# A conformer convolution stage: first projection with its output channel by channel, taps from its second block on, a layer norm of other pieces

## The chip, the cores and the metric

The kernel runs on one core of a Trainium2 chip. The metric is the device time of one execution in microseconds (us); the median of some executions is compared. The engines are named as the profile names them: PE (TensorE, its weight loads PEld), DVE (VectorE), ACT (ScalarE), POOL (GpSimd), SP (SyncE, which issues most DMAs).

## The reference, cut to what matters

A trunk of two layers works on 256 positions of 1024 channels in float32: retention and a dense SwiGLU in layer 0, a conformer convolution module and a mixture of eight experts in layer 1. The change is in the convolution module:

```python
def conv_module(h, w_pw1, b_pw1, w_dw, b_dw, ln_g, ln_b, w_pw2, b_pw2):
    a = h @ w_pw1 + b_pw1
    u = a[..., :D_MODEL] * jax.nn.sigmoid(a[..., D_MODEL:])
    u = lax.conv_general_dilated(
        u, w_dw[:, None, :], window_strides=(1,), padding=[(CONV_WIDTH - 1, 0)],
        dimension_numbers=('NWC', 'WIO', 'NWC'), feature_group_count=D_MODEL) + b_dw
    ...
    un = ((uf - mu) * lax.rsqrt(var + EPS) * ln_g.astype(jnp.float32) + ln_b.astype(jnp.float32)).astype(h.dtype)
    return jax.nn.silu(un) @ w_pw2 + b_pw2
```

`w_pw1` is 1024 x 2048, `w_pw2` 1024 x 1024, the depthwise convolution is causal with 31 taps per channel, and `mu` and `var` run over the 1024 channels of a position.

## The kernel before, in words

Every weight matrix streams through SBUF in blocks of 1 MB (128 partitions x 2048 floats). SP loads a block into one of six `raw` buffers (`load`, L283), as soon as `lo` has freed it. ACT rounds it to fp32r (`hi`, L411, into one of three `whi`), DVE takes the difference (`lo`, L706, into `wlo`). Activations are split in the same way into `xh` and `xl`. A product is then three matmuls: hi by hi, lo activation by hi weight, hi activation by lo weight. `hi` waits until PE has finished the block three before it. Each engine's program is a list written out by hand; engines meet at semaphores, so the place of a `hi`, a `lo` or a tap in its engine's list decides when it runs.

The convolution module, in order:

- `residual(2)` and `turn(2)` normalise and transpose the input; `xh_evac` and `xl_evac` make `xh` and `xl` (512 columns at a time, four of each).
- First projection: blocks `B_PW1` to `B_PW1+7`. `columns` (L1176) keeps a piece of `xh` or `xl` as the stationary operand and streams 512 columns of weights, so the output has positions on partitions. 24 matmuls a block.
- `glu(half)` (L928), after four blocks each: DVE adds the bias to the gate (L932) and to the value (L935), ACT takes the sigmoid (L558), DVE multiplies (L939). PE transposes the product to channels on partitions (`u_turn`, L1439), ACT copies it to `uT` (L564).
- Taps: a chunk is 128 channels. DVE does one tap of one chunk per instruction over 256 positions (`tap`, L956 and L958): chunks 0 to 2, 22 taps of chunk 3 and 21 of chunk 4. PE does the other 112 taps as matmuls with a diagonal of weights (L1455), which ACT builds (L578) into eight buffers. DVE adds the two parts of chunks 3 and 4 (L980). `lo` of the first three blocks of the second projection stands between the taps.
- Layer norm over channels: PE sums `y` with a matrix of ones (L1463), DVE scales the mean (L983) and subtracts it (L985), ACT squares (L600), PE sums the squares the same way (L1467), DVE takes the diagonal of the result and scales it (L988 to L991), POOL takes the power -1/2 (L369), ACT builds two diagonals (L603), PE spreads them over the partitions (L1471), DVE multiplies (L994), ACT does Silu with gain and bias (L606) and copies to `xh` (L608), DVE makes `xl` (`vl`, L905).
- Second projection: `rows` (L1187, L1196, L1197, L1203), four blocks of 24 matmuls of 512 columns; per tile t, hi parts and then lo parts. A block waits for two chunks of `xl` (L1474). In the last block `half_down` is signalled when tile 0 is complete.
- `residual(3)` (L859):

```python
                for t in range(TILES):
                    if t == 0:
                        dve.wait_ge(half_down, n)
                    else:
                        dve.wait_ge(pe_done, used)
                    ...
                        last = nc.vector.tensor_tensor(res[:, t, cols], banks[t][h][:, :], res[:, t, cols], ALU.add)
                    last.then_inc(res_done, 1)
                    if t == 0:
                        mean_square(n, 0)
```

`mean_square` (L711) waits for ACT's sum of squares (L404). Behind it come the normalisation, the transposes (L1267), the router (L1485, matmuls of 8 columns) and the experts, whose rows are gathered by matmuls with a one-hot matrix of 128 columns (L1501, L1502).

## Time and profile before

| | |
|---|---|
| median of 3 runs | 1724.94 us (1723.87 to 1728.66) |
| the profiled execution | 1721.76 us, of which the span of the profile is 1720.0 us |
| busy: PE, PEld | 1619.3 us (94%), 1311.2 us (76%) |
| busy: DVE, ACT, POOL | 1250.5 us (73%), 1024.5 us (60%), 161.6 us (9%) |
| from HBM | 448.61 MB, 261 GB/s over the span |
| mean granted clock of TensorE | 0.978 |

Busy time is the share of the whole span; the convolution module lies between about 467 and 608 us. A matmul's end is modelled, so the distance between the starts of two matmuls says more than the duration of one. The granted clock is given in parts of the full level, 2.4 GHz; 0.50 is the lower level, 1.2 GHz. The trace leaves out some records, so counts in a short stretch can be a little low, and a float32 matmul has two records. The time of the profiled execution holds 1.76 us that lie around its span.

### The profile page before, as it was taken

The page shows a single profiled execution, that of the slowest core. Times are in us where ns is not written, and L with a number is a line of the kernel's source. Part 1 is how long each engine was busy: PE and PEld are TensorE (multiplying, and loading weights), DVE is VectorE, ACT ScalarE, POOL GpSimd, SP SyncE. Part 2 cuts the span into 40 slices and gives each one's busy share as a digit, 9 for nine tenths or more (in the row PEclk, how much of TensorE's full clock was granted, in tenths as well). Part 3 has the DMA queues.
Part 4 walks back from the last instruction along what each step waited for, and adds up shares of the span by engine and source line. Part 5 has one row for each costly group of instructions (what it writes and reads, how often), then busy time and mean ns, then how long its engine had stood idle before and what let it go on. Part 6 is the DMA issues. An engine that isn't in the chain of part 4 may idle for free.

```text
span 1720.0 us, 20864 instructions
## 1 busy us (share of the span) xinstructions
PE 1619.3 (94%) x7325; PEld 1311.2 (76%) x7326; DVE 1250.5 (73%) x1024; ACT 1024.5 (60%) x872; POOL 161.6 (9%) x83
## 2 busy tenths in 40 slices
PE   8999989999899779989999999999999899999996
PEld 6887778888788667767788878878888777777774
DVE  6745554544569559979998888845555499999996
ACT  4344343443349438768777777744444487878874
POOL 0000000000000005006040040010000040330000
PEclk9999999999999869999999999999999899999998
DMA  9653545555442018999999989937666499999994
GB/s 348 208 195 99 182 165 190 195 172 194 175 169 74 25 44 328 393 357 365 397 370 394 371 287 390 373 130 243 207 205 202 148 360 395 374 396 395 375 395 183
DMA packets 191589, 450.23 MB, mean 262 GB/s; under 512 B 8493, under 2 KB 9021, under 8 KB 191422
## 3 DMA queue, kind: packets, MB, share of 16 engines
q1 hardware_dynamic: 189068, 444.83, 71.8%
q10 hardware_dynamic: 2482, 4.85, 0.8%
q8 instruction: 28, 0.46, 0.1%
q14 instruction: 11, 0.09, 0.0%
HBM read 448.61 MB, written 1.05 MB: 261 GB/s over the span
## 4 chain that ended last, share of the span: by engine, by line
PE 63%; DVE 16%; DMA 11%; issue 6%; ACT 3%; DVEq 0%; POOL 0%; ACTq 0%; SPq 0%; POOLq 0%
PE bank L1173 13%; PE bank L1166 12%; PE bank L1167 12%; DVE wlo L706 9%; DMA raw<-in_moe_w_down 6%; DMA raw<-in_moe_w_gu 5%; PE bank L1244 4%; PE bank L1196 3%; PE bank L1203 3%; PE bank L1197 3%; ACT whi L411 3%; DVE y L958 2%; PE bank L1235 2%; PE bank L1236 2%; PE bank L1233 1%
## 5 line engine op out<-in xcount | busy, mean ns | idle before, releaser
L706 DVE TENSOR_TENSOR wlo<-raw,whi 128x2048 fp32r<-128x2048 f32 x422 | 959.6, 2289 | 304.5 <-ACT whi L411 304.1
L411 ACT ACTIVATE whi<-raw 128x2048 fp32r<-128x2048 f32 x422 | 806.5, 1916 | 434.8 <-PE bank L1173 261.9
L1166 PE MATMUL bank<-whi,xx 128*128 128x512 f32 x1152 | 459.2, 399 | 15.1 <-DVE xx L1082 8.7
L1167 PE MATMUL bank<-whi,xx 128*128 128x512 f32 x1152 | 452.8, 393 | 0.0
L1173 PE MATMUL bank<-wlo,xx 128*128 128x512 f32 x1488 | 403.9, 393 | 6.3 <-DVE wlo L706 6.1
L1173 PEld LDWEIGHTS bank<-wlo,xx 128*128 128x128 f32 x1488 | 277.8, 189 | 75.0 <-DVE wlo L706 17.7
L1166 PEld LDWEIGHTS bank<-whi,xx 128*128 128x128 f32 x1152 | 219.5, 191 | 62.2 <-issue 11.2
L1167 PEld LDWEIGHTS bank<-whi,xx 128*128 128x128 f32 x1152 | 219.2, 190 | 44.2
L378 POOL TENSOR_SCALAR onehot<-mats,slot 128x64 fp32r<-128x64 f32 x56 | 150.4, 2709 | 757.9 <-PE bank L1508 757.9
L1244 PE MATMUL bank<-wlo,hT 128*128 128x512 f32 x504 | 143.8, 407 | 16.7 <-DVE wlo L706 14.3
L1244 PEld LDWEIGHTS bank<-wlo,hT 128*128 128x128 f32 x504 | 90.5, 189 | 59.1 <-DVE wlo L706 42.5
L507 ACT ACTIVATE hT<-bank 128x512 fp32r<-128x512 f32 x77 | 44.2, 593 | 96.4 <-PE bank L1385 55.0
L1233 PE MATMUL bank<-whi,hT 128*128 128x512 f32 x336 | 92.3, 397 | 4.4 <-DVE hT L891 4.4
L1164 PE MATMUL bank<-whi,xx 128*128 128x512 f32 x336 | 90.1, 390 | 0.0
L891 DVE TENSOR_TENSOR hT<-bank,hT 128x512 fp32r<-128x512 f32 x77 | 51.5, 683 | 41.5 <-ACT hT L507 41.4
L1233 PEld LDWEIGHTS bank<-whi,hT 128*128 128x128 f32 x336 | 63.3, 190 | 19.3 <-issue 3.8
L1164 PEld LDWEIGHTS bank<-whi,xx 128*128 128x128 f32 x336 | 63.1, 188 | 13.4
L885 DVE TENSOR_TENSOR hid<-bank,sgate 128x512 f32<-128x512 f32 x77 | 51.5, 684 | 20.6 <-PE bank L1173 20.6
L1235 PE MATMUL bank<-whi,hT 128*128 128x512 f32 x168 | 65.9, 392 | 0.0
L1236 PE MATMUL bank<-whi,hT 128*128 128x512 f32 x168 | 65.8, 392 | 0.0
L354 POOL TENSOR_TENSOR rstd<-ms,mhalf 128x1 f32<-128x1 f32 x10 | 6.0, 598 | 513.1 <-DVE ms L711 513.1
L958 DVE SCALAR_TENSOR_TENSOR y<-uT,wdwT,y 128x256 f32<-128x256 f32 x131 | 52.4, 475 | 0.0
(214 smaller groups left out, 1294.3 us busy)
## 6 DMA issues: line engine op xcount, KB each, us to landing
raw<-in_moe_w_gu SPq DMA_DIRECT2D x224, 1024.0 KB, 8.2
raw<-in_moe_w_down SPq DMA_DIRECT2D x112, 1024.0 KB, 8.6
raw<-in_ffn_w_gu SPq DMA_DIRECT2D x28, 1024.0 KB, 5.1
raw<-in_ret_w_in SPq DMA_DIRECT2D x24, 1024.0 KB, 7.2
raw<-in_ffn_w_down SPq DMA_DIRECT2D x14, 1024.0 KB, 4.9
raw<-in_conv_w_pw SPq DMA_DIRECT2D x12, 1024.0 KB, 5.1
raw<-in_ret_w_out SPq DMA_DIRECT2D x8, 1024.0 KB, 4.9
res<-in_x SPq DMA_DIRECT2D x2, 512.0 KB, 4.1
```

Source lines behind the costliest of these rows:

```text
L378: last = nc.gpsimd.tensor_scalar(onehot[:, n // 2, at_:at_ + HALF], iota[:, h * HALF:(h + 1) * HALF], slot[:, e + 1, n, h:h + 1], None, AL ...
L411: nc.scalar.activation(whi[base % SPLIT][:, :], raw[base % RAW][:, :], ACT.Copy).then_inc(hi_done, 1)
L706: nc.vector.tensor_tensor(wlo[base % SPLIT][:, :], raw[base % RAW][:, :], whi[base % SPLIT][:, :].bitcast(f32), ALU.subtract).then_inc(lo_ ...
L958: ins = nc.vector.scalar_tensor_tensor(y[:, c, :], uT[:, c, k:k + SEQ], w, y[:, c, :], ALU.mult, ALU.add)
L1164: nc.tensor.matmul(dst[:, :], xmix[:, kc, t, :], wh, start=kc == 0, stop=False)
L1166: nc.tensor.matmul(dst[:, :], xh[:, kc, t, :], wh, start=kc == 0, stop=False)
L1167: nc.tensor.matmul(dst[:, :], xl[:, kc, t, :], wh, start=False, stop=False)
L1173: last = nc.tensor.matmul(dst[:, :], both, wl, start=False, stop=closing and kc == DC - 1)
L1233: nc.tensor.matmul(dst, hTmix[:, kc, t, :], wh, start=False, stop=False)
L1235: nc.tensor.matmul(dst, hTh[:, kc, t, :], wh, start=False, stop=False)
L1236: nc.tensor.matmul(dst, hTl[:, kc, t, :], wh, start=False, stop=False)
L1244: last = nc.tensor.matmul(dst, both, wl, start=False, stop=stop and c == 1)
```

## The change

- The first projection keeps a 128 x 128 piece of the weights stationary and streams the 256 positions of `xh` or `xl` (`channels`), so its output has channels on partitions. A pair of blocks gives four chunks of output, two of values and two of gates, in four banks; the loads are cut in two so that a block holds both. A block is 48 matmuls of 256 columns. The first waits for all four pieces of `xh`, and for `xl` only after its first 16 matmuls.
- The transposes, the copies to `uT`, the bias broadcast and the bias adds go. ACT takes the sigmoid from PSUM with the bias as its operand; DVE adds the bias, multiplies, and writes `uT` in one instruction per chunk (`glu`). These happen per pair of blocks.
- DVE takes whole chunks 0 to 4 (155 taps), PE whole chunks 5 to 7 (93 taps). DVE's first taps come after `glu(0)`; its order of taps, `lo` and `glu` is new. The three `lo` of the second projection move from between the taps to behind them: `lo(B_PW2)` before the mean, the next two between the multiplies of the layer norm.
- Layer norm: the sums use a matrix of 1/D, four of the eight mean sums are made during PE's taps, DVE subtracts straight from PSUM. For the variance the squares are the stationary operand and one column of 1/D streams. A one-element Silu is placed ahead on ACT.
- Second projection: the matmuls of a block are ordered by chunk, hi parts of both tiles first and lo parts last, with waits per chunk of `xh` and `xl`.

The diff, cut to its core (the names, semaphores and index expressions that go with it are left out):

```diff
-EARLY_TAPS = 7
-VECTOR_TAPS = {0: TAPS, 1: TAPS, 2: TAPS, 3: 22, 4: 21}
+VECTOR_CHUNKS = 5
+QUARTER = D // 4
...
+        sig = at("sig", [P, 4, SEQ], f32, conv_at)
...
-        PE_TAPS = [(c, k) for c in range(DC) for k in range(VECTOR_TAPS.get(c, 0), TAPS)]
-        PE_FIRST = TAPS - VECTOR_TAPS[3]
+        PE_TAPS = [(c, k) for c in range(VECTOR_CHUNKS, DC) for k in range(TAPS)]
+
+        def pw1_bank(q):
+            return 4 * ((q + 1) % 2)
...
+                    sp.dma_start(small[3 * DC:5 * DC, :], conv_b_pw1[0].rearrange("(c p) -> c p", p=P)).then_inc(L["small"], 16)
...
-            for n in range(4):
-                for half in range(2):
-                    load(B_PW1 + 2 * n + half, cols(conv_w_pw1[0], half, (n // 2 + 2 * (n % 2)) * BANK))
+            for b in range(8):
+                q, half = b // 2, b % 2
+                sp.wait_ge(lo_done, B_PW1 + b - RAW + 1)
+                slot_ = (B_PW1 + b) % RAW
+                for g in range(2):
+                    col = g * D + q * QUARTER
+                    sp.dma_start(raw[slot_][:, :].rearrange("p (c g n) -> p c g n", c=4, g=2)[:, :, g, :],
+                                 conv_w_pw1[0, half * 512:(half + 1) * 512, col:col + QUARTER]
+                                 .rearrange("(c p) n -> p c n", p=P)).then_inc(arrived[slot_], 16)
...
-            act.dma_start(mats[:, 1:5, :], c_mats[:, 1:5, :]).then_inc(L["mats"], 16)
+            act.dma_start(mats[:, 1:6, :], c_mats[:, 1:6, :]).then_inc(L["mats"], 16)
...
-            act.dma_start(bias1[:, :], conv_b_pw1[0].partition_broadcast(P)).then_inc(L["bias1"], 16)
...
-            glu_evac(0)
+            def gate_sigmoid(q):
+                act.wait_ge(pe_done, B_PW1 + 2 * q + 2)
+                for m in range(2):
+                    c = 2 * q + m
+                    nc.scalar.activation(sig[:, c % 4, :], bank[pw1_bank(q) + 2 + m][:, 0:SEQ], ACT.Sigmoid,
+                                         bias=smallT[:, 4 * DC + c:4 * DC + c + 1]).then_inc(sig_done, 1)
+
+            hi(B_PW1 + 2)
+            hi(B_PW1 + 3)
+            hi(B_PW1 + 4)
+            gate_sigmoid(0)
             hi(B_PW1 + 5)
             hi(B_PW1 + 6)
-            uT_evac(0)
+            gate_sigmoid(1)
             hi(B_PW1 + 7)
...
             for m in range(8):
                 build(m)
-            glu_evac(1)
...
+            gate_sigmoid(2)
+            hi(B_PW2)
+            gate_sigmoid(3)
+            for m in range(8, len(PE_TAPS)):
                 build(m)
...
+                if k == 10 and c < 7:
+                    hi(B_PW2 + c - VECTOR_CHUNKS + 1)
+                if k == 8 and c > VECTOR_CHUNKS:
+                    tap_out(c - 1)
+            tap_out(7)
+            nc.scalar.activation(warm[:, 0:1], smallT[:, 0:1], ACT.Silu)
...
+            def glu(q):
+                for m in range(2):
+                    c = 2 * q + m
+                    dve.wait_ge(sig_done, c + 1)
+                    nc.vector.scalar_tensor_tensor(uT[:, c, PAD:PAD + SEQ], bank[pw1_bank(q) + m][:, 0:SEQ],
+                                                   smallT[:, 3 * DC + c:3 * DC + c + 1], sig[:, c % 4, :],
+                                                   ALU.add, ALU.mult).then_inc(u_done, 1)
...
+            glu(0)
+            lo(B_PW1 + 4)
+            for k in range(7):
+                if k == 4:
+                    lo(B_PW1 + 5)
+                tap(0, k)
+                tap(1, k)
             glu(1)
...
+            lo(B_PW1 + 6)
+            for k in range(5):
+                if k == 3:
+                    lo(B_PW1 + 7)
+                tap(0, 7 + k)
+                tap(2, k)
+                tap(1, 7 + k)
+                tap(3, k)
+            glu(2)
+            for k in range(8):
+                tap(0, 12 + k)
+                tap(1, 12 + k)
+                tap(2, 5 + k)
+            glu(3)
...
+            tap(3, 30)
+            lo(B_PW2)
             dve.wait_ge(mu_ps, 1)
-            own(nc.vector.tensor_scalar(mean[:, :], bank[0][:, 0:SEQ], 1.0 / D, None, ALU.mult))
             for c in range(DC):
-                nc.vector.tensor_tensor(y[:, c, :], y[:, c, :], mean[:, :], ALU.subtract).then_inc(yc_done, 1)
+                nc.vector.tensor_tensor(y[:, c, :], y[:, c, :], bank[0][:, 0:SEQ], ALU.subtract).then_inc(yc_done, 1)
             dve.wait_ge(var_ps, 1)
-
-            own(nc.vector.tensor_tensor(diag[:, 2:4, :], bank[1][:, 0:SEQ].rearrange("p (t n) -> p t n", t=TILES),
-                                        ident.unsqueeze(1).to_broadcast([P, TILES, P]), ALU.mult))
-            own(nc.vector.reduce_sum(lnv[:, 1, :], diag[:, 2:4, :], AX.X))
-            nc.vector.tensor_scalar(lnv[:, 0, :], lnv[:, 1, :], 1.0 / D, EPS, ALU.mult, ALU.add).then_inc(var_sb, 1)
+            for t in range(TILES):
+                last = nc.vector.tensor_scalar(lnv[:, 0, t:t + 1], bank[1 + t][:, 0:1], EPS, None, ALU.add)
+            last.then_inc(var_sb, 1)
...
                 if c >= 2:
                     vl(c - 2)
+                if c in (4, 6):
+                    lo(B_PW2 + c // 2 - 1)
...
+            def channels(q, half):
+                base = B_PW1 + 2 * q + half
+                acc = [bank[pw1_bank(q) + m][:, 0:SEQ].rearrange("p (t n) -> p t n", t=TILES) for m in range(4)]
+                pe.wait_ge(hi_done, base + 1)
+                if base == B_PW1:
+                    pe.wait_ge(xh_done, 12)
+                for m in range(4):
                     for c in range(4):
...
+                        kc, wh = 4 * half + c, whi[base % SPLIT][:, c * BANK + m * P:c * BANK + (m + 1) * P]
+                        nc.tensor.matmul(acc[m], wh, xh[:, kc, :, :], start=kc == 0, stop=False)
...
+            for q in range(4):
+                if q >= 2:
+                    pe.wait_ge(u_done, 2 * q - 2)
+                for half in range(2):
+                    channels(q, half)
...
+                if (c, k) == (7, 12):
+                    pe.wait_ge(u_done, 8)
+                    pe.wait_ge(tap_seq, 91)
+                    mean_sum(0, True, False)
+                    mean_sum(1, False, False)
+                    for n in range(2):
+                        pe.wait_ge(y_pe, n + 1)
+                        mean_sum(VECTOR_CHUNKS + n, False, False)
...
+            pe.wait_ge(tap_seq, TAPS * VECTOR_CHUNKS)
+            for c in range(2, VECTOR_CHUNKS):
+                mean_sum(c, False, False)
+            pe.wait_ge(y_pe, 3)
+            mean_sum(7, False, True).then_inc(mu_ps, 1)
             for c in range(DC):
                 pe.wait_ge(sq_done, c + 1)
-                last = nc.tensor.matmul(bank[1][:, 0:SEQ], ones, sq[:, c, :], start=c == 0, stop=c == DC - 1)
+                for t in range(TILES):
+                    last = nc.tensor.matmul(bank[1 + t][:, 0:1], sq[:, c, t * P:(t + 1) * P], share[:, 0:1],
+                                            start=c == 0, stop=c == DC - 1)
...
             for r in range(4):
-                pe.wait_ge(vl_done, 2 * r + 2)
-                rows(B_PW2 + r, xh, xl, 2 * r, r == 0, r == 3)
+                base = B_PW2 + r
+                pe.wait_ge(hi_done, base + 1)
+                for c in range(2):
+                    kc = 2 * r + c
+                    for part, ready in ((xh, vh_done), (xl, vl_done)):
+                        pe.wait_ge(ready, kc + 1)
+                        for t in range(TILES):
+                            for n in range(2):
+                                nc.tensor.matmul(DOWN[t][n][:, :], part[:, kc, t, :],
+                                                 whi[base % SPLIT][:, c * D + n * BANK:c * D + (n + 1) * BANK],
+                                                 start=kc == 0 and ready is vh_done, stop=False)
+                pe.wait_ge(lo_done, base + 1)
+                for t in range(TILES):
+                    for c in range(2):
+                        for n in range(2):
+                            last = nc.tensor.matmul(DOWN[t][n][:, :], xh[:, 2 * r + c, t, :],
+                                                    wlo[base % SPLIT][:, c * D + n * BANK:c * D + (n + 1) * BANK],
+                                                    start=False, stop=r == 3 and c == 1)
+                    if r == 3 and t == 0:
+                        last.then_inc(half_down, 1)
+                last.then_inc(pe_done, 1)
```

## Rows read from the trace of the kernel before

**Rows 1.** The page, part 4: the chain that ended last, share of the span by engine.

```profile
PE 63%; DVE 16%; DMA 11%; issue 6%; ACT 3%; DVEq 0%; POOL 0%; ACTq 0%; SPq 0%; POOLq 0%
```

**Rows 2.** Busy time by stretch: PE, PEld, DVE, ACT, POOL, granted clock, DMA share, GB/s.

```profile
512.00:566.00 54.00, 51.21 (x240) 44.33 (x238) 53.18 (x118) 43.80 (x114) 0.00 (x0) 1.00 0.18 59
```

**Rows 3.** The chain in order of time, layer norm: start us, us, what.

```profile
566.82 4.50 PE bank L1463 x12
...
572.74 3.73 PE bank L1467 x16
576.50 0.44 DVE diag L988
...
577.66 0.71 POOL lnv L369
...
579.10 1.28 ACT L606
580.40 0.61 ACT y L606
581.03 0.42 ACT xx L608
...
582.90 0.80 PE bank L1196
```

**Rows 4.** Timeline of PE and PEld in the gather (start, us); last, the chain's projection.

```profile
745.47 0.31 PE L1501 MATMUL bank<-onehot,zh 128*128 128x128 f32 x1
...
748.96 0.27 PE L1502 MATMUL bank<-onehot,zl 128*128 128x128 f32 x1
...
748.90 0.19 PEld L1502 LDWEIGHTS bank<-onehot,zl 128*128 128x128 f32 x1
...
475.66 0.91 PE bank L1173 x4
```

**Rows 5.** Timeline of ACT, start of the first projection.

```profile
467.52 0.60 ACT L417 ACTIVATE xx<-bank 128x512 fp32r<-128x512 f32 x1 [0.26 <-PE bank L1267]
...
479.38 1.92 ACT L411 ACTIVATE whi<-raw 128x2048 fp32r<-128x2048 f32 x1 [3.52 <-PE bank L1173]
481.32 1.28 ACT L558 ACT_TABLE_LOAD   x1
```

**Rows 6.** DVE at the first taps (timeline), and lo and taps (chain).

```profile
501.21 1.38 DVE L956 TENSOR_SCALAR y<-uT,wdwT,smallT 128x256 f32<-128x256 f32 x4
...
525.72 2.20 DVE wlo L706
527.92 9.90 DVE y L958 x25
```

**Rows 7.** PE's taps alone (L1455) in a stretch of 10 us, by stretch.

```profile
530.00:540.00 10.00, 10.00 (x48) 1.00 0.25 95
```

**Rows 8.** PE and its granted clock in slices of 1 us, by stretch.

```profile
468.00:469.00 1.00, 1.00 (x4) 0.55 0.22 14
...
567.00:568.00 1.00, 1.00 (x5) 0.94 0.00 0
...
571.00:572.00 1.00, 0.31 (x1) 0.85 0.00 0
```

**Rows 9.** Timeline of PE, the router's matmuls of 8 columns.

```profile
613.32 6.83 PE L1485 MATMUL bank<-wr,hT 128*128 128x8 f32 x32
```

**Rows 10.** Timeline of DVE, residual behind the second projection.

```profile
604.82 1.29 DVE L867 TENSOR_TENSOR res<-bank,res 128x512 f32<-128x512 f32 x2 [3.79 <-PE bank L1203]
607.32 0.15 DVE L711 TENSOR_SCALAR ms<-ss 128x1 f32<-128x1 f32 x1 [1.22 <-ACT z L404]
607.54 1.29 DVE L867 TENSOR_TENSOR res<-bank,res 128x512 f32<-128x512 f32 x2
```

**Rows 11.** ACT's copy of raw block 2 (timeline), PE's first matmul on it (chain).

```profile
22.29 1.92 ACT L411 ACTIVATE whi<-raw 128x2048 fp32r<-128x2048 f32 x1 [5.84 <-DMA raw<-in_ret_w_in]
...
26.09 0.44 PE bank L1166
```

More of the change, by code:

```diff
@@ L74, in trunk @@
         gains = at("gains", [P, 2, D], f32)
-        mats = at("mats", [P, 5, P], f32)
-        ident, earlier, ones, iota, fold = (mats[:, i, :] for i in range(5))
-        small = at("small", [24, P], f32)
-        smallT = at("smallT", [P, 24], f32)
+        mats = at("mats", [P, 6, P], f32)
+        ident, earlier, ones, iota, fold, share = (mats[:, i, :] for i in range(6))
+        small = at("small", [40, P], f32)
+        smallT = at("smallT", [P, 40], f32)
         wdw = at("wdw", [124, 2, P], f32)
```

154 lines of the change are left out of this document (53 added, 101 removed).

## The prediction

> **What bounds the kernel now.** I read the profile's page first. The share list of the chain that ended last gives PE 63% and DVE 16% [rows 1]: over the whole run TensorE decides, but the change touches one stage only, so the question is which engine ends last there. The table by stretch answers for 512 to 566 us: the granted clock is 1.00, PE is busy 51.2 and DVE 53.2 of 54 us [rows 2]. The chain in order of time then runs DVE, PE, DVE, ACT, PE, DVE, POOL, ACT from 566.8 to 582.9 us, one short piece behind another [rows 3]: the taps of the depthwise convolution end on DVE, the mean begins on PE at 566.82, and the second projection can begin at 582.90. The conv stage is therefore a DVE chain (taps), then a latency chain (layer norm), then PE again. Work that only makes DVE's taps start or end earlier is worth its full length, up to the point where PE's taps end last.
>
> **First projection: the same TensorE time, I think.** Before, a block is 24 matmuls of 512 columns, four in 0.91 us, so 0.2275 each and 5.46 us a block. After, it is 48 of 256 columns, each with a weight load of its own. No row has this form. The nearest rows are the gather's, fp32r with 128 columns, and the f32 transposes: 32 gather matmuls from 745.47 to 748.96 us, 3.49/31 = 0.1126 us each at full clock [rows 4]. Lower bound: half of the 512-column one less its overhead, about 0.107. Upper bound: the duration of one weight load, 0.19 us, as the load row beside the gather shows it. I take 0.113, since 0.1126 already contains a load that is hidden behind a shorter stream, and half of 0.2275 is 0.114 too. The projection is then 384 x 0.113 = 43.4 us against 192 x 0.2275 = 43.7 us. The sixteen transposes (L1439) go from PE, but the first matmul now waits for all four hi copies of the normalised rows; the last one runs from 467.52 to 468.12 [rows 5], and it began about when PE's first matmul did, so the start moves by 0.65 us. The clock was at half level there [rows 8]; I allow 0.8 us for it, an estimate. PE leaves the projection at 468.1 + 0.8 + 43.4 = 512.3 us.
>
> The Trainium skill, page TensorE: Matmul & The Clock Gate, speaks against this part: its section Part 3: Packing small matmuls — row/col tiling has a weight load overlap running matmuls only when the row group differs, and its section LDWEIGHTS (loading the stationary operand) gives 107 ns for 128 columns; one after the other that would be an estimated 0.21 us a matmul and 39 us more. The trace disagrees: a load of 0.19 us and a stream of 512 columns fit together in 0.2275 us [rows 4].
>
> **Start of the taps.** Before, the first tap is at 501.21 us [rows 6], behind four blocks, DVE's bias adds, a sigmoid and transposes. After, the sigmoid reads PSUM once two blocks are done. ACT's hi copy behind the end of block 1 starts at 479.38; with the shift 480.0, it ends at 482.0; the table load of 1.28 us [rows 5] now stands on the path, then a sigmoid of 256 columns, 0.6 like the Silu of that size [rows 3]: 483.9. DVE's two gated products (0.45 each, from taps of the same size) end at 484.7. From there DVE never waits, as far as I can follow it. The tightest place is the second pair of sigmoids: block 3 ends at 490.7, ACT's copy (1.9) and two sigmoids (1.2) end at 493.8, and DVE, after 14 taps and two lo, gets there at 494.6. Its work to the last tap: lo(4) to lo(7), 4 x 2.2 = 8.8; six more products, 2.7; 155 taps of 0.396 (25 in 9.90 us) = 61.4 [rows 6]. Sum 72.9: the last tap ends at 557.6. The adds of PE's partial chunks (L980) are gone. Before, the mean could begin at 566.82 [rows 3], so the gain is 9.2 us. The two-chunk loops make each tap depend on the one two back; that one is done 0.3 us before it is needed, so I cost it at nothing.
>
> **TensorE's taps.** 93 instead of 112. The stretch 530 to 540 holds 48 records at two per tap [rows 7], about 47 whole ones, 0.426 us a tap: 512.3 + 39.6 + four early mean sums of 0.45 = 553.7 us. DVE remains last by 3.9 us; that slack covers the 0.65 us and any pitch up to 0.123.
>
> **Layer norm.** Before, 12 records of the mean ran from 566.82 for 4.50 us, mostly at half clock [rows 3]: the granted clock fell at 567.9, after PE had waited 2.7 us for DVE, and rose in the slice 571 to 572 [rows 8]. Now PE waits 3.9 us, so I expect the fall again. Eight records of 512 cycles at 1.2 GHz are 3.4 us (1.8 at 2.4 GHz): mean at 561.1. lo(B_PW2), 2.2 us, moved behind the taps, is hidden under this at half clock, and costs 0.3 us at full clock. Subtract and square, 0.9: PE starts the variance at 562.0. It was 16 records of 256 columns in 3.73 us at full clock. It becomes 32 records with one column, all load. The nearest row is the router's, 8 columns, 32 records in 6.83 us at half clock [rows 9], and the gather gives 32 x 0.1126 = 3.6 us at full clock [rows 4]. The router's 6.8 us of steady small matmuls did not raise the clock, so I take half clock: 568.8. So here the new form gives nothing at full clock and costs 3.1 us at half clock. Then two one-column adds, 0.3, instead of the 1.16 us from L988 to POOL; POOL, two diagonals, two matmuls 2.3 (2.1 before, plus 0.2 for the clock); multiply 0.41, Silu 0.60 without the table load that held it until 580.38, copy 0.42. The second projection starts on xh of chunk 0, no longer on xl of chunk 1. Sum: 568.8 + 0.3 + 2.3 + 1.5 = 572.9 against 582.9 [rows 3]: gain 10.0 us.
>
> **Second projection and the residual.** The same 96 matmuls. They took from 582.90 to 607.54 us, 24.6, where 96 x 0.2275 is 21.8: the start at half clock is in it, and I leave it there. lo of blocks 1 and 2 (2.2 us each) now stands between DVE's multiplies; block 1 needs xl(3) 8 us after the start and gets it by 6.7, so nothing there. But the reordered block 3 signals the first half only 4 matmuls (0.91 us) before its end instead of 12 (2.73). DVE adds at 604.82 (1.29), waits 1.22 for ACT's square, computes the mean square (0.15), and only then may add the second half, at 607.54, just when PE ended [rows 10]. Behind a signal that is 1.82 us later relative to PE's end, the second add, and all that follows, waits 1.8 us. This is a **new stall**.
>
> **Cost elsewhere.** The 1 MB bias broadcast goes; loads of the first projection become two DMAs of 512 KB each with 1 KB rows. The queue was waiting on lo, and the tightest, block 7, has over 20 us between issue and use. 64 KB more constants and one small DMA at the start delay raw block 2 by 0.5 us, an estimate; its hi copy ran from 22.29 to 24.2, and PE came to it at 26.09 [rows 11]. Both nothing. MoE loads wait for lo of B_PW2, now at 560 to 575 us, still 60 us ahead of their use.
>
> **Sum.** 10.0 - 1.8 = 8.2 us. The profiled execution took 1721.76 us (span 1720.0), the median is 1724.94; it gives 1713.6 for that execution and 1716.7 for the median, rounded to 1716.5.
>
> **Rivals.**
> A, as above: 1716.5 us.
> B, the clock stays or is back at full level for the sums and the variance. For: it rose at 571 behind the mean's matmuls [rows 8]. Mean 1.6 less, variance 3.2 less, diagonals 0.2, but lo(B_PW2) takes 0.3 back: gain 12.8, 1712; if the second projection starts at full clock too, up to 2.8 more, 1709.
> C, most of the gain is lost to clock phases: the start at 468.1 stays at half level for as long again as the stretch 567.9 to 571.3 (3.4 us, 1.7 of them lost, ahead of DVE's chain), the second projection too (1.7), the chain behind the residual loses another 1: gain 3.8, 1721. For: the projection does start at half level [rows 8]. Against: all must go wrong together.
> D, slower: the weight load becomes the bound of the 256-column matmul. At 0.19 us the projection is 73 us and ends at 542, the taps and sums at 583.4; 25.8 us later than DVE, so 17.6 us slower, 1742.5. It decides from 0.144 us a matmul (12 us of slack and gain over 384). Against: 0.1126 in the gather. Its worse form, the load in front of the stream and not beside it, is 0.19 + 0.107 = 0.30 us, 41 us more, 1783. By the Trainium skill's rule on row groups (same page and section as above) this is what would come; rows 4 contradict it, and I give it 0.01 of D's chance.
> That the change does not do what it says would be a first tap that is not earlier, because ACT is late with the sigmoid; it was idle for 3.52 us before its copy at 479.38 [rows 5], so I give it little.
>
> **Chances.** A 0.48, B 0.28, C 0.16, D 0.05, and 0.03 for that last case with a result like the old one. 0.3% is 5.2 us, about what a measurement of this kernel can tell. Some of C's spread lies beyond it on the fast side, and D with small overruns elsewhere on the slow one: faster 0.80, same 0.13, slower 0.07. The range runs from B with a full-clock second projection to C: 1708.0 to 1721.5.
>
> **What would show it.** Right: first tap near 485 us; projection matmuls 0.113 us apart; last tap near 557.5; PE idle for about 4 us before the last sums; variance 6.8 us; 1.8 us more between the end of the second projection and the last residual add. Wrong: a pitch over 0.123, PE's taps ending after DVE's, DVE waiting for ACT between products, or full clock through the variance.

## The result, and the profile after

| | before | after |
|---|---|---|
| median | 1724.4 us (1723.58 to 1728.66, 4 runs) | 1707.0 us (1704.48 to 1710.39, 4 runs) |
| ratio, 95% interval | | 0.9901 [0.9884, 0.9918] |
| profiled execution, its span | 1721.76, 1720.0 us | 1710.39, 1708.6 us |
| busy: PE, DVE, ACT | 1619.3, 1250.5, 1024.5 us | 1609.9, 1251.6, 1019.9 us |

The kernel is 17.4 us faster by the medians, 11.4 us by the two profiled executions; the profiled execution before is faster than all four that were timed, the one after is the slowest of its four. The forecast was 8.2 us. The sign was right, the size was not.

The chain of the kernel after, in order of time, through the layer norm (start us, us, what; it answers to [rows 3]):

```profile
558.13 2.20 DVE wlo L708
560.33 0.34 DVE y L997
...
561.16 4.97 PE bank L1501 x32
566.15 0.23 DVE lnv L1000 x2
566.46 0.71 POOL lnv L373
...
569.36 0.61 ACT y L608
569.99 0.42 ACT xx L610
570.55 5.38 PE bank L1518 x16
```

The mean's wait is gone from the chain: `lo` (L708) ends at 560.33 and DVE subtracts at once. The variance follows as 32 records. No table load stands before Silu, and PE starts the second projection at 570.55, right behind the first copy to `xh`.

PE's timeline in the first projection (one third of a block, and the start of the next), and then around the mean, with its idle time in brackets:

```profile
473.06 2.08 PE L1465 MATMUL bank<-xx,wlo 128*128 128x256 f32 x16
474.98 2.08 PE L1454 MATMUL bank<-xx,whi 128*128 128x256 f32 x16
```

```profile
554.82 2.54 PE L1490 MATMUL bank<-uT,diag 128*128 128x256 f32 x11
558.18 1.99 PE L1475 MATMUL bank<-y,mats 128*128 128x256 f32 x8 [0.83 <-DVE y L951]
561.16 4.95 PE L1501 MATMUL bank<-mats,sq 128*128 128x1 f32 x32 [0.98 <-ACT sq L602]
```

Sixteen matmuls of 256 columns start 1.92 us before the next sixteen, 0.120 us each. PE's taps end at 557.36, DVE's last tap at 558.1, so PE waited 0.83 us and not the 3.9 us of the forecast. The eight records of the mean took 1.99 us: full clock.

DVE's timeline (it answers to [rows 6] and [rows 10]):

```profile
484.83 0.88 DVE L935 SCALAR_TENSOR_TENSOR uT<-bank,smallT,sig 128x256 f32<-128x256 f32 x2 [5.36 <-ACT sig L562]
...
487.82 0.73 DVE L949 TENSOR_SCALAR y<-uT,wdwT,smallT 128x256 f32<-128x256 f32 x2
...
532.85 25.28 DVE L951 SCALAR_TENSOR_TENSOR y<-uT,wdwT,y 128x256 f32<-128x256 f32 x63
...
593.19 1.29 DVE L869 TENSOR_TENSOR res<-bank,res 128x512 f32<-128x512 f32 x2 [4.57 <-PE bank L1525]
595.69 0.15 DVE L713 TENSOR_SCALAR ms<-ss 128x1 f32<-128x1 f32 x1 [1.22 <-ACT z L408]
595.76 1.28 DVE L869 TENSOR_TENSOR res<-bank,res 128x512 f32<-128x512 f32 x2
```

The first gated product starts at 484.83, the first tap at 487.82, and from there DVE is never idle until 558. At the end of the stage the second residual add starts at 595.76, behind ACT's square of the first half; PE had ended at 594.1.

PE and its granted clock in slices of 1 us (it answers to [rows 8]):

```profile
558.00:559.00 1.00, 0.82 (x4) 1.00 0.00 0
...
561.00:562.00 1.00, 0.84 (x8) 1.00 0.46 55
...
563.00:564.00 1.00, 1.00 (x8) 0.72 1.06 410
...
573.00:574.00 1.00, 1.00 (x5) 0.66 0.00 0
```

The clock is at full level through the mean, falls at 563.4 in the middle of the one-column matmuls, and rises again at 573.7, three microseconds into the second projection. In the kernel before it rose 5.5 us into it (582.9 to 588.4).

**Where the gain lies.** Four marks divide an execution: the start of the residual add of the second half (tile 1) in `residual(2)`, at the end of layer 0 (called the first mark below), that of `residual(3)`, the first gathered rows of the experts (L1082 before, L1094 after), the end. Three traces of the kernel before and four of the kernel after (its own and the repeats below), in us:

| stretch | before | after | mean gain | forecast |
|---|---|---|---|---|
| start to `residual(2)` | 461.3, 463.6, 461.1 | 462.8, 461.7, 461.8, 461.3 | 0.1 | 0 |
| to `residual(3)`: the changed stage | 146.2, 146.2, 146.2 | 133.0, 134.6, 133.0, 135.3 | 12.3 | 8.2 |
| router, to the first gathered rows | 28.8, 28.8, 28.8 | 25.9, 29.0, 25.9, 25.9 | 2.1 | 0 |
| experts | 1083.6, 1087.4, 1087.1 | 1086.9, 1079.2, 1077.0, 1080.2 | 5.2 | 0 |

The sum of the mean gains is 19.7 us before rounding, a little above what the ratios of the kernel after and its repeats give (0.9907 to 0.9889, 16 to 19 us). So about 4 us of the surplus lie inside the stage and 7.3 behind it.

### The profile page after: what moved, and what is told of

It is laid out like the page before. It is cut to its first block, busy times and chain, and to the rows that moved or that the text cites. A ratio compares the mean times of both kernels' runs of the same rounds, so it can differ in the third digit from the quotient of the medians.

```text
span 1708.6 us, 21171 instructions
## 1 busy us (share of the span) xinstructions
PE 1609.9 (94%) x7479; PEld 1314.1 (77%) x7480; DVE 1251.6 (73%) x1035; ACT 1019.9 (60%) x854; POOL 151.8 (9%) x83
## 4 chain that ended last, share of the span: by engine, by line
PE 61%; DVE 16%; DMA 12%; issue 6%; ACT 4%; DVEq 0%; ACTq 0%; POOL 0%; SPq 0%; POOLq 0%
PE bank L1185 12%; PE bank L1178 12%; PE bank L1179 12%; DVE wlo L708 9%; DMA raw<-in_moe_w_down 8%; DMA raw<-in_moe_w_gu 4%; PE bank L1256 4%; DVE y L951 3%; ACT whi L418 3%; PE bank L1208 2%; PE bank L1215 2%; PE bank L1209 2%; PE bank L1247 2%; PE bank L1248 2%; PE bank L1245 1%
## 5 line engine op out<-in xcount | busy, mean ns | idle before, releaser
L708 DVE TENSOR_TENSOR wlo<-raw,whi 128x2048 fp32r<-128x2048 f32 x422 | 960.2, 2288 | 299.8 <-ACT whi L418 299.5
L1178 PE MATMUL bank<-whi,xx 128*128 128x512 f32 x1088 | 435.2, 400 | 15.7 <-DVE xx L1094 8.7
L1179 PE MATMUL bank<-whi,xx 128*128 128x512 f32 x1088 | 429.4, 395 | 0.0
L1185 PE MATMUL bank<-wlo,xx 128*128 128x512 f32 x1424 | 387.0, 394 | 7.6 <-DVE wlo L708 7.6
L1185 PEld LDWEIGHTS bank<-wlo,xx 128*128 128x128 f32 x1424 | 266.4, 189 | 74.3 <-DVE wlo L708 18.5
L1178 PEld LDWEIGHTS bank<-whi,xx 128*128 128x128 f32 x1088 | 207.8, 191 | 59.9 <-issue 12.5
L1179 PEld LDWEIGHTS bank<-whi,xx 128*128 128x128 f32 x1088 | 207.7, 191 | 41.9
L382 POOL TENSOR_SCALAR onehot<-mats,slot 128x64 fp32r<-128x64 f32 x56 | 140.6, 2536 | 761.7 <-PE bank L1563 761.7
L1176 PE MATMUL bank<-whi,xx 128*128 128x512 f32 x336 | 89.9, 389 | 0.0
L1176 PEld LDWEIGHTS bank<-whi,xx 128*128 128x128 f32 x336 | 63.1, 188 | 13.3
L951 DVE SCALAR_TENSOR_TENSOR y<-uT,wdwT,y 128x256 f32<-128x256 f32 x150 | 60.3, 480 | 0.1
```

What stands on the lines that cost most here:

```text
L382: last = nc.gpsimd.tensor_scalar(onehot[:, n // 2, at_:at_ + HALF], iota[:, h * HALF:(h + 1) * HALF], slot[:, e + 1, n, h:h + 1], None, AL ...
L708: nc.vector.tensor_tensor(wlo[base % SPLIT][:, :], raw[base % RAW][:, :], whi[base % SPLIT][:, :].bitcast(f32), ALU.subtract).then_inc(lo_ ...
L951: ins = nc.vector.scalar_tensor_tensor(y[:, c, :], uT[:, c, k:k + SEQ], w, y[:, c, :], ALU.mult, ALU.add)
L1176: nc.tensor.matmul(dst[:, :], xmix[:, kc, t, :], wh, start=kc == 0, stop=False)
L1178: nc.tensor.matmul(dst[:, :], xh[:, kc, t, :], wh, start=kc == 0, stop=False)
L1179: nc.tensor.matmul(dst[:, :], xl[:, kc, t, :], wh, start=False, stop=False)
```

## The experiments

Every run is compared with the kernel before on its own chip. The recorded texts set theories against each other: by CLOCK a time follows the granted clock, which differs between executions; by WORK it belongs to the work of the change itself; by DRAW it is spread between executions.

### Repeats: a_again, b_again, a_third, b_third, a_fourth

No edit. The texts on record:

> The changed kernel once more, for a second trace. Its first trace is 11.4 us shorter than the one of before (1708.6 against 1720.0 us of span), its median 17.4 us. Between the second residual add of the first layer and the first expert it gained 16.1 us where 8.2 were forecast. Theory CLOCK: the surplus is what TensorE's granted clock does in the sparse stretches, and it differs between executions: the median is 1704 to 1710 us again, but the second projection, the router or the start of the experts take a time that differs by 1 to 3 us from the first trace. Rival WORK: the surplus belongs to the change's own work; every one of these stretches repeats within 0.5 us.

> The kernel before once more, for a second trace. Its first trace belongs to an execution of 1721.76 us, less than every other one of this kernel (1722.8 to 1728.7). CLOCK: this trace is 2 to 5 us longer, and the surplus sits in sparse stretches where the granted clock is at half level, or in the experts. Rival WORK: all stretches up to the experts repeat within 0.5 us.

> The changed kernel a third time, beside the kernel before on the same chip, to place the gain. The traces so far give 11.6 to 13.2 us for the stretch between the two residual adds and 0 to 3 us more for the router; the medians gave 17 to 20 us on two chips. Theory DRAW: the rest is spread of the experts' part, which took 1079 to 1088 us in the traces whatever the kernel: here the gain is 12 to 17 us, and the part from the first expert on differs from the kernel before by less than 2 us. Rival WORK: the change shortens the experts' part too, by about 4 us.

> The kernel before a third time, on the same chip as the run above. DRAW: the part from the first expert on takes the same as in that run within 2 us. WORK: it takes about 4 us more.

> The changed kernel a fourth time, as the measure for the three runs beside it. Three traces of either kernel now put 12.7 us of the mean gain between the residual adds, 1.9 in the router and 5.0 in the experts' part, which ran 1077 to 1087 us against 1084 to 1087. CLOCK: the experts' part differs by which quiet places between experts begin or end at half clock; it comes out anywhere from 1077 to 1088 us again. Rival WORK: it is below 1082 us again because the change altered something there.

Measured: a_again 1706.2 us, 0.9889 [0.9870, 0.9907]; b_again one execution of 1727.8 us; a_third 1705.1 us, 0.9907 [0.9885, 0.9929]; b_third 1723.5 us, 1.0006 [0.9994, 1.0018]; a_fourth 1704.6 us, 0.9890 [0.9868, 0.9911]. Their traces are in the table above. The kernel before repeats its stage and its router to 0.1 us; the kernel after varies by 2.3 and 3.1 us. The experts' part varies in both, but lies lower after in three of four traces. So DRAW alone, as a_third and b_third were asked, is wrong on that chip (1077.0 against 1087.1), though this pair sets the fastest execution of a_third (1699.5 us, median 1705.1) against one of the slower ones of b_third; and WORK fails on the router and the stage, which do not repeat. The 1080.2 us of a_fourth fit both of its texts.

Two causes of the spread inside the stage can be read. In a_again the clock fell at 562.1 and rose only at 575.7, 5.9 us into the second projection and not 3.1, so more of the variance and of the projection ran at half clock. The other is in a_fourth. PE and its clock at the start of the first projection of a_fourth:

```profile
468.00:470.00 2.00, 1.77 (x8) 0.50 0.31 26
...
472.00:474.00 2.00, 2.00 (x17) 0.94 0.79 242
```

Here the projection began at half clock and stayed there until about 472, which delays the first tap by 2.4 us (27.4 against 25.0 us behind the first mark) and all that follows. It is the first term of rival C, and it came in four traces of the changed kernel and its variants (a_fourth, a_rows, a_switch, a_all).

### Fewer taps on PE: a_less

```diff
-        PE_TAPS = [(c, k) for c in range(VECTOR_CHUNKS, DC) for k in range(TAPS)]
+        PE_TAPS = [(c, k) for c in range(VECTOR_CHUNKS, DC) for k in range(TAPS) if not (c == 7 and 14 <= k < 22)]
```

> The changed kernel without 8 of PE's 93 taps (taps 14 to 21 of chunk 7 are left out of the convolution). PE then waits for DVE's last tap for 0.8 + 3.4 = 4.2 us, as the prediction had it with a matmul of 0.113 us. CLOCK: the granted clock falls at or before the mean's sums, which take 3.8 us and not 2.0; DVE's first subtraction comes 1.5 to 2 us later although less work is done. The variance may fall into a full-clock stretch. Rival: an idle PE costs nothing, the sums take 2.0 us and the subtraction starts as early as before.

PE's timeline, and two slices of its clock:

```profile
549.79 3.18 PE L1490 MATMUL bank<-uT,diag 128*128 128x256 f32 x14
557.25 3.78 PE L1475 MATMUL bank<-y,mats 128*128 128x256 f32 x8 [4.28 <-DVE y L951]
561.99 6.98 PE L1501 MATMUL bank<-mats,sq 128*128 128x1 f32 x32 [0.96 <-ACT sq L602]
```

```profile
555.00:556.00 1.00, 0.00 (x0) 0.80 0.00 0
...
560.00:561.00 1.00, 1.00 (x3) 0.50 0.42 39
```

Here PE has the slack of the prediction. It waits 4.28 us, the clock falls at 555.6, the mean's sums take 3.78 us, the variance 6.98 (forecast 6.8), and the stage takes 138.2 us; the prediction's terms give 607.54 - 8.2 - 461.3 = 138.0. With 8 taps more, PE's wait is 0.83 us and the stage is 133.0 to 134.6 us in the three traces whose first tap comes as early. **Less work on PE made the stage 3.6 to 5.2 us longer.** The whole time (1607.6 us) can't be compared: without these taps the values differ, and the experts' part shrinks to 976.9 us.

### Later first taps: a_late

```diff
             glu(0)
             lo(B_PW1 + 4)
-            for k in range(7):
-                if k == 4:
-                    lo(B_PW1 + 5)
-                tap(0, k)
-                tap(1, k)
+            lo(B_PW1 + 5)
             glu(1)
+            for k in range(7):
+                tap(0, k)
+                tap(1, k)
```

> The changed kernel with its first 14 taps behind the second pair of gated products (that is, behind four blocks, as before the change) and not behind the first. By the prediction DVE is the engine that ends last in this stage, so every microsecond that it idles shows: DVE then waits from the end of lo(5) to the sigmoids of the second pair, 5 to 6 us less their overlap; last tap 5 us later, whole time 1708 + 4 = 1711 to 1713 us. Rival: PE is now the bound (its matmuls take 0.120 us, its taps ended only 0.8 us before DVE's), and has slack for nothing: then it is the same 5 us, but with PE idle before the mean; if instead the taps' start is not what decides, the time stays within 1 us of the changed kernel.

1710.4 us, 0.9930 [0.9905, 0.9955]. The last tap ends 100.1 us behind the first mark and not 95.4: 4.8 us. DVE is the bound, as predicted. The first subtraction is 6.5 us later, though (104.0 against 97.5), and PE's timeline tells why:

```profile
563.58 3.78 PE L1474 MATMUL bank<-y,mats 128*128 128x256 f32 x8 [5.62 <-DVE y L951]
```

PE waited 5.62 us, the clock fell, and the mean took 3.78 us again. The stage is 139.5 us, 6.5 more than the 133.0 of the trace after: a microsecond of DVE costs more than a microsecond here.

### The variance as before: a_var

```diff
-                for t in range(TILES):
-                    last = nc.tensor.matmul(bank[1 + t][:, 0:1], sq[:, c, t * P:(t + 1) * P], share[:, 0:1],
-                                            start=c == 0, stop=c == DC - 1)
+                last = nc.tensor.matmul(bank[1][:, 0:SEQ], share, sq[:, c, :], start=c == 0, stop=c == DC - 1)
...
-            for t in range(TILES):
-                last = nc.vector.tensor_scalar(lnv[:, 0, t:t + 1], bank[1 + t][:, 0:1], EPS, None, ALU.add)
-            last.then_inc(var_sb, 1)
+            own(nc.vector.tensor_tensor(diag[:, 2:4, :], bank[1][:, 0:SEQ].rearrange("p (t n) -> p t n", t=TILES),
+                                        ident.unsqueeze(1).to_broadcast([P, TILES, P]), ALU.mult))
+            own(nc.vector.reduce_sum(lnv[:, 1, :], diag[:, 2:4, :], AX.X))
+            nc.vector.tensor_scalar(lnv[:, 0, :], lnv[:, 1, :], EPS, None, ALU.add).then_inc(var_sb, 1)
```

> The changed kernel with the variance summed as before: 16 records of 256 columns and the diagonal taken on DVE. CLOCK: the one-column matmuls are what lets the granted clock fall at 563.7 us; with 256 columns the sum takes 3.7 us and not 5.0, DVE takes 0.9 us more, the clock stays up into the second projection, which is 1.5 to 2 us shorter: 1 to 3 us faster in all. WORK: the form has no bearing on the clock, the second projection starts at half clock as well, and the kernel is 0 to 1 us slower.

1703.6 us, 0.9875 [0.9857, 0.9892], beside 0.9889 for a_again on the same chip: the intervals overlap. PE's timeline and its clock:

```profile
560.26 3.72 PE L1501 MATMUL bank<-sq,mats 128*128 128x256 f32 x16 [0.98 <-ACT sq L602]
566.36 1.22 PE L1505 MATMUL bank<-diag,mats 128*128 128x128 f32 x4 [2.39 <-ACT diag L605]
569.27 5.58 PE L1517 MATMUL bank<-whi,xx 128*128 128x512 f32 x16 [1.68 <-ACT xx L610]
```

```profile
563.00:564.00 1.00, 0.98 (x5) 1.00 0.98 381
...
565.00:566.00 1.00, 0.00 (x0) 1.00 0.00 0
566.00:567.00 1.00, 0.64 (x3) 0.50 0.00 0
```

The sum took 3.72 us at full clock, so the one-column form (4.9 to 5.2 us in the three traces with the same first tap) does cost 1.2 to 1.5 us at the clock it gets. But the clock fell all the same, at 566.0, while PE waited from 564.0 to 566.4 for the chain of DVE, POOL and ACT, and the second projection started at half clock. Half of CLOCK's expectation failed: the form of the sum decides its own length, the quiet chain behind it takes the clock. The second projection starts 0.3 to 0.7 us earlier than in the three traces of the changed kernel that had the same first tap; that is all that this trace shows for the form.

### The order of the second projection: a_tail, a_rows, b_rows

a_tail puts the last block alone back into the old order:

```diff
-            for r in range(4):
+            for r in range(3):
                 base = B_PW2 + r
...
+            pe.wait_ge(vl_done, 8)
+            rows(B_PW2 + 3, xh, xl, 6, False, True)
```

> The changed kernel with only the last block of the second projection in the old order, so that the first half of the output is signalled 12 matmuls ahead of the end and not 4. Both theories: the second residual add starts within 0.1 us of PE's end and not 1.8 us behind it, 1.8 us less in the stretch. In the whole time 1.8 us less, unless the clock of the router's stretch gives some back.

DVE's timeline at the end of the stage:

```profile
591.58 1.29 DVE L869 TENSOR_TENSOR res<-bank,res 128x512 f32<-128x512 f32 x2 [2.84 <-PE bank L1215]
594.09 0.15 DVE L713 TENSOR_SCALAR ms<-ss 128x1 f32<-128x1 f32 x1 [1.22 <-ACT z L408]
594.30 1.29 DVE L869 TENSOR_TENSOR res<-bank,res 128x512 f32<-128x512 f32 x2
```

The signal comes at 591.58, 2.7 us ahead of PE's end at 594.3, and the second add starts at 594.30. In the kernel after it waited from 594.1 to 595.76. The stage is 131.3 us, 1.7 to 3.3 less than in the traces with the same first tap. The new stall of the prediction is shown, at 1.7 us for 1.8. Median 1703.7 us, 0.9882 [0.9862, 0.9901], against 0.9889 for a_again: the intervals overlap, and in its trace the router took 29.0 us, as in a_again.

a_rows puts all four blocks back in the changed kernel, b_rows gives the new order to the kernel before:

```diff
-            for r in range(4):
-                base = B_PW2 + r
...
+            for r in range(4):
+                pe.wait_ge(vl_done, 2 * r + 2)
+                rows(B_PW2 + r, xh, xl, 2 * r, r == 0, r == 3)
```

> The changed kernel with the second projection's matmuls in their old order (tile by tile, a block waits for two chunks of xl). CLOCK: the start moves 1.4 us later, the 1.8 us stall before the second residual add goes, so within 2 us of the changed kernel, and PE's end of the projection is met by the add at once. WORK: the new order was worth more than its forecast; the kernel is 3 us slower or more than the changed one.

> The kernel before with the new order of the second projection alone. The prediction's terms: the start 1.4 us earlier, the second residual add 1.8 us later relative to PE's end: within 1 us of the kernel before (1723 to 1727 us). Rival WORK, that this order brings part of the surplus: 3 us faster or more.

a_rows: 1706.8 us, 0.9893 [0.9877, 0.9910]; a_again beside it 0.9889. Its stage is 136.0 us against the 135.3 of a_fourth, which had the same slow start. b_rows: 1721.0 us, 1.0000 [0.9983, 1.0018]; its stage is 145.7 us against 146.2. The new order is worth 0.5 to 0.8 us of the stage, one pair of traces each, and nothing that the whole time shows: what it gains at the start it all but gives back at the end, in both kernels.

The router tells something else here. Its 32 matmuls in the trace after, in b_rows and in a_tail:

```profile
601.36 4.12 PE L1540 MATMUL bank<-wr,hT 128*128 128x8 f32 x32
```

```profile
615.64 4.01 PE L1504 MATMUL bank<-wr,hT 128*128 128x8 f32 x32
```

```profile
600.27 6.83 PE L1541 MATMUL bank<-wr,hT 128*128 128x8 f32 x32
```

The clock came back just before them in the first two (at 601.0 and 615.3) and not in the third, and the router's stretch is 25.9, 25.9 and 29.0 us. So the kernel before, with a stage as long as ever, got the fast router of the kernel after, and the shorter stage of a_tail did not.

### PE kept busy: a_fill_var, a_switch, b_switch, a_all

Matmuls of zeros by zeros, into banks that nothing reads, stand where PE waits. For a_fill_var, on top of a_var:

```diff
+            def keep_busy(count, where):
+                for _ in range(count):
+                    nc.tensor.matmul(where[:, :], zeros[:, 0:P], zeros[:, :], start=True, stop=True)
...
             last.then_inc(var_ps, 1)
+            pe.wait_ge(moe_set, 4)
+            keep_busy(6, bank[7])
...
             last.then_inc(lnb_ps, 1)
+            keep_busy(7, bank[7])
...
+            keep_busy(13, bank[3])
             turn(3)
...
             last.then_inc(lg_ps, 1)
+            keep_busy(11, bank[6])
...
+            keep_busy(15, bank[6])
...
             gather(0, 0).then_inc(gather_ps, 1)
+            keep_busy(9, bank[7])
```

> The changed kernel with the variance summed as before and with matmuls of zeros by zeros, 512 columns each, into banks that are free, where PE has nothing to do: 6 and 7 in the layer norm, 13 behind the second projection, 11 and 15 in the router, 9 behind the gather. CLOCK: the granted clock then stays at full level from the mean to the experts: the second projection begins at full clock (2 us less), router 2.7 us less where it was at half clock, gather 3.3 us, the first blocks of the experts 2.5 us: 8 to 10 us faster than the changed kernel. Rival WORK: these stretches do not hang on what PE did before them, or the added matmuls delay what is behind them: no gain or a loss of 1 to 3 us.

1707.9 us, 0.9924 [0.9898, 0.9951]. In its trace the stage is 130.7 us (a_var 132.8) and the router 24.0 (25.9), so 4 us are gained where the matmuls stand. The clock stayed at full level from the mean to 599.6 and was at half level from there to 606.5, through most of the router's matmuls (5.45 us). The experts' part is 1088.0 us, and no gain is left over a_again's ratio, taken on another chip: the 8 to 10 us expected did not come. One expert took 121.3 us there and 113 to 114 in all other traces, which I can't explain.

a_switch and b_switch have 24 such matmuls behind each expert whose rows fill two tiles; it happens once with these inputs:

```diff
                 expert_rows(B_MOE + 41, 2, True, kind, need, six)
+                if kind == WIDE:
+                    keep_busy(24, bank[3])
```

> The changed kernel with 24 matmuls of zeros by zeros, 512 columns, behind every expert whose rows fill two tiles; there PE waits 6.6 us for DVE and then computes the next expert's first gates at half clock (7.3 us in the changed kernel's trace, 8.4 in that of before, 5.5 at full clock). CLOCK: the first gates behind such an expert take 5.5 us, 2 to 3 us less for each, 2 to 5 us less in all. Rival: DVE, ACT and the DMA queues set the pace there, and nothing changes; or the added matmuls end behind the gathered rows and cost 1 us each.

> The kernel before with the same 24 matmuls behind every expert of two tiles. CLOCK: its experts' part gains as much as that of a_switch or, if the changed kernel owed its shorter part to a higher clock, 1 to 3 us more: 3 to 7 us faster than before. WORK: the difference of the experts' parts (about 4 us) stays.

a_switch: 1705.1 us, 0.9881 [0.9859, 0.9904], beside 1704.6 us and 0.9890 for a_fourth, so the 2 to 5 us expected do not show in the whole time. b_switch: 1720.3 us, 0.9980 [0.9964, 0.9996], about 3.5 us less than the kernel before. The chain at that place, from the first gate matmul to the end of the second block, in the kernels before, after and b_switch:

```profile
1360.59 0.79 PE bank L1166
...
1369.12 0.01 PE bank L1210
```

```profile
1348.22 0.79 PE bank L1178
...
1355.69 0.01 PE bank L1222
```

```profile
1361.86 0.49 PE bank L1166
...
1367.61 0.34 PE bank L1523
```

8.5, 7.5 and 5.75 us (a_switch 5.7), and the matmuls are the same. The granted clock there, by stretch, in the same three traces:

```profile
1357.00:1366.00 9.00, 5.41 (x13) 0.50 0.49 145
```

```profile
1346.00:1351.00 5.00, 2.78 (x7) 0.50 0.55 175
```

```profile
1362.00:1368.00 6.00, 6.00 (x27) 1.00 0.80 260
```

How long the half level lasts makes the difference: 10.2 us before, 6.8 after, none with the added matmuls. The stretch between two experts that holds this place is 221.0, 221.2 and 221.0 us in the three traces before, 219.0 to 219.4 in the four after, and 218.3 and 217.7 in b_switch and a_switch. So of the 5.2 us in the experts 1.9 lie in this stretch: 1.3 are the clock, and 0.6 remain when it is held up in both kernels. The experts' parts of b_switch and a_switch are 1080.4 and 1081.0 us: the difference of 5 us is gone in this pair. One pair, against a spread of 10 us, does not settle the rest.

The 0.6 us are no accident of the draw. From the one-hot matrix of an expert to the first gathered rows of the next, this stretch takes 203.4 us in all five traces of the kernel before and its variants, and 202.8 to 202.9 in every trace of the changed kernel and its variants that computes the same experts; two others take 107.0 to 107.1 and 106.7 to 106.8. One of these, before and after:

```profile
885.80:992.80 107.00, 106.82 (x500) 1.00 1.01 375
```

```profile
871.50:978.20 106.70, 106.52 (x500) 1.00 1.01 375
```

PE is busy throughout, at full clock, with as many matmuls. The three make 1.2 us of the gain in the experts. The change alters no instruction there; it makes three tiles of constants larger (`mats`, `small`, `smallT`), which moves what lies behind them in SBUF. No run tests whether that is the reason.

a_all joins the old variance, the edit of a_tail and all the added matmuls.

> The changed kernel with the variance as before, the last block of the second projection in the old order, the matmuls of zeros in the layer norm, behind the second projection, in the router and behind the gather, and those behind the experts of two tiles. CLOCK: from the first residual add to the first expert 155 to 156 us less the 1.8 of the order: about 153; experts' part 1075 to 1082: 5 to 9 us faster than the changed kernel. Rival: the experts' part is bound by its transfers and takes back what the start gains: within 3 us of the changed kernel.

**1697.5 us, 0.9831 [0.9806, 0.9855]**, beside 1704.6 us and 0.9890 for a_fourth: 7 us faster than the changed kernel and 29 faster than the one before by its ratio. PE's timeline:

```profile
570.93 3.88 PE L1524 MATMUL bank<-whi,xx 128*128 128x512 f32 x16
...
592.77 3.12 PE L1448 MATMUL bank<-zeros 128*128 128x512 f32 x13
...
598.54 3.71 PE L1548 MATMUL bank<-wr,hT 128*128 128x8 f32 x32
```

The first 16 matmuls of the second projection take 3.88 us (5.38 in the trace after) and the router's 3.71: the clock stayed at full level until 602.6. It was at half level for 3.4 us behind the router's matmuls, in spite of the added ones, and back by the gather. Stage 131.4 us, with the slow start of a_fourth (135.3); router 22.3 us (25.9); experts 1081.7 us (1080.2). What is gained ahead of the experts was kept here.

Last, a_var_tail joins the edits of a_var and a_tail, without added matmuls:

> The changed kernel with both cures: variance in 256 columns as before, last block of the second projection in the old order. Each alone was 2.5 us under the changed kernel by the median on its chip. Together 3 to 5 us faster than the changed kernel of this call: second residual add at 130.5 to 131.5 us behind that of the first layer, against 133 to 134.6.

1705.3 us, 0.9903 [0.9881, 0.9924], beside 0.9907 for a_third. Its stage is 131.2 us, as expected, 1.8 less than in a_third's trace, but router and experts came out longer (29.1 and 1082.6) and the whole did not move. The expected 3 to 5 us are not shown.

## Why the prediction was right and wrong

**First projection.** "I take 0.113" was too low: 0.120 us at full clock. It was inside the bounds given (0.107 to 0.19) and inside the 0.123 that the slack was said to cover. The block takes 5.76 us and not 5.46, 2.7 us for all eight. The start gave 1.2 us back: it came 6.4 us behind the first mark and not 7.6, since in three of the four traces the clock was at full level there. So PE left the projection 1.5 us later than forecast. By itself this cost nothing, as said; rival D, its worse form included, is out. The Trainium skill, page TensorE: Matmul & The Clock Gate, section Back-to-back issue gap, gives 262 cycles for 256 columns, an estimated 0.109 us at full clock; the 0.120 us measured here are 288.

**The step that failed** is "DVE remains last by 3.9 us" together with "Now PE waits 3.9 us, so I expect the fall again". I used that slack to cover the pitch, and did not ask what using it up would do to the clock. PE left the projection 1.5 us later, its taps took 0.7 us more, and DVE's last tap came 1.0 us earlier. So PE waited 0.8 us, the clock stayed up through the mean, and fell in the middle of the variance. a_less gives PE the slack again and with it the predicted stage, 138.2 us for 138.0. The stage is 134.0 us in the mean of four: 4 us of the error. In the trace after, the 5.1 us that are missing are 1.0 of DVE's last tap, 1.4 of the mean, 1.8 of the variance and 1.2 of the second projection, where the prediction left the half-clock start of the kernel before; the chain between variance and projection took 0.3 more.

**Start of the taps, DVE's chain: right.** First tap forecast with lo(4) at 486.9 us, measured 487.8 in an execution whose first mark stood 1.5 us later. Last tap 96.3 us behind the first mark by the forecast, 95.4 measured. a_late shows that DVE decides.

**Layer norm.** Shorter tail of the variance, no table load, start on chunk 0: right, PE starts the second projection 4.4 us behind the variance (forecast 4.1). Variance 4.8 to 5.2 us in the four traces of the changed kernel for 6.8.

**Residual stall: right.** 1.7 us for 1.8, shown by a_tail.

**Router and experts.** The sum had nothing for them, apart from C, which feared a loss of 1 us, and gave no reason why they would stay as they were. The traces show a mean gain of 2.1 us in the router and 5.2 us in the experts. The router's 32 matmuls took 4.0 to 4.1 us in three of four traces (6.8 in a_again and before), because the clock had come back just ahead of them. That the shorter stage brings this is not shown: b_rows had it with a stage of 145.7 us, a_tail and a_var_tail, with 131.3 and 131.2, did not. Of the experts' 5.2 us, 1.3 are the clock behind the expert of two tiles, and 1.2 are the three stretches that run faster at full clock.

Rival B at 1709 us was nearest; my range ended 1 us above the measured median. The mechanism of B holds for the mean; for the variance only in part, and the router and the experts were not in it. That B came so near the whole time is partly luck.

Open: nearly 3 us of the experts' shorter part, part of which may be the draw of the traces; why the experts' code runs 1.2 us faster at full clock; and what decides whether the clock is up for the router. Clock levels at the other changes of expert differ between traces as well; no run here takes them away one by one.

## What to carry to other kernels

Slack of TensorE ahead of a short dependent chain is not free: if PE waits long enough for the granted clock to fall, the matmuls of the chain cost up to double (the mean's sums 3.78 us for 1.99). Balance engines so that PE arrives just before the last one, or fill the wait with matmuls that nothing reads. And when a stage changes, follow the clock into the code behind it, and take several traces of both kernels: two executions differed here by more than most terms of the sum.

## What was not expected of the hardware

- In these traces a 256-column fp32r matmul with its own weight load runs every 0.120 us, a 128-column one every 0.113, a 512-column one every 0.2275, all at full clock.
- PE busy in the profile does not mean that the clock stays or rises. It fell during the 32 back-to-back one-column matmuls in all four traces of the changed kernel, and the 6.8 us of the router's did not raise it in the kernel before. With matmuls of 512 columns of zeros by zeros in the waits it stayed up from 472.9 to 602.6 us in a_all, and the mean granted clock of the whole run was 0.985 against 0.976 in a_fourth; it still fell once, for 3.4 us, in the router.
- The same kernel's projection began at full clock in some executions and at half in others, worth 2.4 us at the first tap.
- Two stretches of the experts whose instructions the change does not alter, busy on PE at full clock, took 106.7 to 106.8 us in every trace of the changed kernel and its variants with the same experts, and 107.0 to 107.1 in every one of the kernel before and its variants.
